# A hybrid attention, convolution and memory layer on eight cores: the first token blocks, the row sums' banks, the order of the key groups, and two seams

## The reference

```
z = x @ w_in                                  # q, k, v, f, g_fox, B, C, h, g_conv, mq, g_mem
logf = log_sigmoid(f + fox_bf)                # per head, 12 heads x 128
o_fox  = softmax(q.k/sqrt(128) + cum_t - cum_s, causal) @ v     # sample: 1024 cached keys before its own
o_conv = B * conv3(C * h)                     # causal, depthwise, 1536 channels, 2 steps of state
o_mem  = softmax(mq.mk/16) @ mv               # 4 heads x 256, 256 memory tokens
y_i = (o_i * silu(g_i)) @ w_i_out             # three branches
m = sum_i sigmoid(x @ w_merge_i + b_i) * y_i
y = LayerNorm(2**0.25 * x + m @ w_o)
```

## Time and profile before

| | us |
|---|---|
| median of 3 runs | 3396.12 (3395.94 to 3399.55) |
| profiled execution | 3396.83 |
| its span on the slowest core | 3395.1 |
| PE busy | 3283.1 (97%) |
| DVE, ACT, POOL busy | 1227.6, 906.3, 847.0 |
| mean granted PE clock, cores | 0.990 to 0.992 |

### The profile page before, as it was taken

The page is one execution under the profiler, slowest core; times in us unless marked ns, Lnnn a source line. Parts: engine busy times, 40 slices in busy tenths (PEclk is TensorE's granted clock), DMA queues, the critical chain, the costliest instruction groups (busy, mean ns, idle before and its releaser), DMA issues.

```text
span 3395.1 us, 54170 instructions; the slowest of 8 cores (3386.3 to 3395.1 us)
## 1 busy us (share of the span) xinstructions
PE 3283.1 (97%) x18645; PEld 1638.8 (48%) x18998; DVE 1227.6 (36%) x2041; ACT 906.3 (27%) x1572; POOL 847.0 (25%) x1046
## 2 busy tenths in 40 slices
PE   6999999999998999999999999999999999999998
PEld 3555555555544444444444444445544444444443
DVE  0477777777775222222211111111102331111465
ACT  0355555555553111111111111111113331111111
POOL 2233333333333222222200000222221113222233
PEclk8999999999999999999999999999999999999999
DMA  9554534343432121212134433866661115665543
GB/s 156 101 98 81 88 75 83 73 86 75 82 61 39 30 44 32 41 35 37 36 83 108 109 89 90 177 144 144 150 150 30 25 26 130 138 145 144 199 160 124
DMA packets 156405, 315.76 MB, mean 93 GB/s; under 512 B 32784, under 2 KB 60048, under 8 KB 151708
## 3 DMA queue, kind: packets, MB, share of 16 engines
q0 software_dynamic: 43840, 134.54, 24.1%
q1 hardware_dynamic: 112296, 177.73, 17.8%
HBM read 351.42 MB, written 95.32 MB: 132 GB/s over the span
## 4 chain that ended last, share of the span: by engine, by line
PE 92%; DMA 3%; issue 2%; DVE 1%; ACT 1%; POOL 0%; DVEq 0%; ACTq 0%; POOLq 0%; SPq 0%
PE bank L146 92%; DMA xT<-xTp 1%; DMA m_scr<-mt 1%; DVE st L181 0%; DMA fk_p<-k 0%; DVE acc L173 0%; ACT k L168 0%; DMA wcb<-wcM 0%; ACT rl L163 0%; DVE rr L181 0%; PE bank L149 0%; ACT sc L163 0%; ACT ge L163 0%; DVE pt L173 0%; POOL wv L155 0%
## 5 line engine op out<-in xcount | busy, mean ns | idle before, releaser
L146 PE MATMUL bank<-xT,wcb 128*128 128x512 bf16 (+1 forms) x3757 | 715.2, 342 | 9.8 <-DMA wcb<-wcM 4.7
L146 PE MATMUL bank<-xT,cwb 128*128 128x512 bf16 (+1 forms) x3766 | 693.9, 342 | 3.9 <-issue 0.2
L146 PE MATMUL bank<-xT,wkqg 128*128 128x512 bf16 (+1 forms) x2812 | 595.7, 344 | 18.3 <-DMA wkqg<-wkqg 5.9
L173 DVE TENSOR_TENSOR mt<-bank,gt 128x512 f32<-128x512 f32 (+1 forms) x240 | 143.6, 598 | 1033.8 <-PE bank L146 940.0
L146 PEld LDWEIGHTS bank<-xT,wcb 128*128 128x128 bf16 x3840 | 326.8, 98 | 366.9 <-issue 8.1
L146 PEld LDWEIGHTS bank<-xT,cwb 128*128 128x128 bf16 x3840 | 324.0, 98 | 362.4 <-issue 4.3
L163 ACT ACTIVATE pt<-st,ncc 128x512 bf16<-128x512 f32 (+4 forms) x492 | 318.7, 649 | 396.4 <-DVE st L181 306.6
L163 ACT ACTIVATE gt<-bank,bm 128x512 f32<-128x512 f32 (+1 forms) x240 | 147.1, 613 | 964.0 <-PE bank L146 959.8
L146 PEld LDWEIGHTS bank<-xT,wkqg 128*128 128x128 bf16 x2880 | 244.6, 98 | 270.7 <-issue 27.6
L181 DVE SCALAR_TENSOR_TENSOR st<-bank,cq 128x512 f32<-128x512 f32 x480 | 291.6, 608 | 172.0 <-PE bank L146 155.3
L173 DVE TENSOR_TENSOR acc<-acc,pt 128x512 f32<-128x512 f32 (+3 forms) x396 | 260.4, 658 | 0.4
(11 more groups left out here) (148 smaller groups left out, 2624.8 us busy)
## 6 DMA issues: line engine op xcount, KB each, us to landing
m_scr<-mt SPq DMA_DIRECT2D x128, 256.0 KB, 2.2
pv<-m_scr SPq DMA_DIRECT2D x128, 256.0 KB, 4.8
cwb<-wc POOLq DMA_DIRECT2D x10, 2048.0 KB, 15.1
mw<-wm POOLq DMA_DIRECT2D x16, 1024.0 KB, 12.2
x<-xp SPq DMA_DIRECT2D x16, 1024.0 KB, 7.0
y_p<-rr SPq DMA_DIRECT2D x16, 1024.0 KB, 4.8
wkqg<-wkqg POOLq DMA_DIRECT2D x40, 384.0 KB, 9.0
wcb<-wcC POOLq DMA_DIRECT2D x16, 896.0 KB, 9.0
```

The costliest lines, as they stand in the source:

```text
L146: return lambda e: e.matmul(out, lhsT=lhsT, rhs=rhs, start=start, stop=stop)
L173: return lambda e: e.tensor_tensor(out=out, in0=in0, in1=in1, op=op)
```

## The change

- Start: blocks 0 and 1 are both computed in seven banks side by side (four v groups, k, q, g), a quarter of the contraction at a time. The weights of head 0's k, q, g come in quarters, each behind the quarter of block 0; blocks 1 and 2 come in quarters. The constants go out from SP behind block 0, the later ones behind block 1; `identb` is dropped, `bfb` has a resource of its own.
- Row sums take their bank from `nextbank()`.
- The groups of the next head have a new order: one or no v group ahead of each, and key groups not next to each other.
- The copy of the sample's conv state goes from POOL to DVE.
- At the end of attention the low part of the last row sum and the first projection group of channel group 1 are put out before the row sum.
- In the last combine the order of the last two items' units is changed.

```diff
-    for t, n in ((identb, "identb"), (identf, "identf"), (onesb, "onesb")):
-        S.add(SP, DMA(t[:], I[n]), writes=[r_const], dmasem=dconst)
...
+    def load_const():
+        for t, n in ((identf, "identf"), (onesb, "onesb")):
+            S.add(SP, DMA(t[:], I[n]), writes=[r_const], dmasem=dconst)
+        S.add(SP, DMA(lcT[:, 0:PAST], I["clfT"]), writes=[r_lc], dmasem=d_clf)
+
+    def load_late():
+        for t, n in ((bm, "b_merge"), (cwT, "conv_w"), (cbT, "conv_b"), (sconvT, "sconv")):
+            S.add(SP, DMA(t[:], I[n]), writes=[r_late], dmasem=dlate)
...
         load_x(0, g, g + 1, S.dmasem(f"x0g{g}"))
-    for g in range(0, 4, 2):
-        load_kw(0, g, g + 2, S.dmasem(f"k0g{g}"))
-    for g in range(0, 4, 2):
-        load_x(1, g, g + 2, S.dmasem(f"x1g{g}"))
-    load_x(2, 0, 2, S.dmasem("x2a"))
-    load_x(2, 2, 4, S.dmasem("x2b"))
+        load_kw(0, g, g + 1, S.dmasem(f"k0g{g}"))
+    for tb in (1, 2):
+        for g in range(4):
+            load_x(tb, g, g + 1, S.dmasem(f"x{tb}g{g}"))
...
+    def stream_block(tb):
+        gs = [(2 + j, v_group(0, tb * 4 + j, True)) for j in range(4)]
+        gs += [(0, k_group(0, tb, True)), (1, q_group(0, tb, raw=True)), (7, g_group(0, tb, raw=True))]
+        for g in range(4):
+            for bk, (mm, ev) in gs:
+                for c in range(g * 4, g * 4 + 4):
+                    mm(bk, c, c == 0, c == 15)
+        for bk, (mm, ev) in gs:
+            ev(bk)
+    stream_block(0)
+    load_const()
+    stream_block(1)
+    load_late()
+    for tc in range(8, 12):
+        run_all(v_group(0, tc))
+    run_all(k_group(0, 2) + q_group(0, 2) + g_group(0, 2))
...
-                    lb = 2 + take("s", 2)
+                    lb = nextbank()
...
-                    S.add(POOL, COPY(conv["us"][:, 0:2], sconvT[:, :, c]), reads=[r_late], writes=[r_us])
+                    S.add(DVE, COPY(conv["us"][:, 0:2], sconvT[:, :, c]), reads=[r_late], writes=[r_us])
...
-            rest = []
-            for tb in (1, 2, 3, 4):
-                if h > 0 or tb > 2:
-                    rest.append(k_group(n, tb))
-                if tb == 1:
-                    rest += [g_group(n, 0, past_block[0]), q_group(n, 1, past_block[1]), g_group(n, 1, past_block[1])]
-            nv = (len(vs) // 4 + len(rest) - 1) // len(rest)
-            for grp in rest:
-                fill += vs[:4 * nv] + grp
-                vs = vs[4 * nv:]
-            assert not vs
-            fill += q_group(n, 4) + g_group(n, 4)
-            for tb in (2, 3):
-                fill += q_group(n, tb, past_block[tb]) + g_group(n, tb, past_block[tb])
+            rest = [k_group(n, 1)] if h > 0 else []
+            rest += [g_group(n, 0, past_block[0]), q_group(n, 1, past_block[1])]
+            rest += [k_group(n, 2)] if h > 0 else []
+            rest += [g_group(n, 1, past_block[1]), k_group(n, 3), q_group(n, 4), g_group(n, 4)]
+            nv, nr = len(vs) // 4, len(rest)
+            for k, grp in enumerate(rest):
+                fill += vs[4 * (nv * k // nr):4 * (nv * (k + 1) // nr)] + grp
+            fill += q_group(n, 2, past_block[2]) + k_group(n, 4) + g_group(n, 2, past_block[2])
+            fill += q_group(n, 3, past_block[3]) + g_group(n, 3, past_block[3])
...
-    for due, fn in later:
+    now[0] = None
+    ps = conv_pieces(1, True)
+    later[0][1]()
+    run_all(ps[:4])
+    for due, fn in later[1:]:
         fn()
...
+    units = [(k, tb) for k in range(len(ITEMS) - 2) for tb in range(5)]
+    ka, kb = len(ITEMS) - 2, len(ITEMS) - 1
+    units += [(ka, 0), (ka, 1), (kb, 0), (ka, 2), (kb, 1), (ka, 3), (kb, 2), (ka, 4), (kb, 3), (kb, 4)]
```

More of the change, by code:

```diff
@@ L217 @@
     ("wo", [4, 128, 16, 512], F32), ("ln_g", [1, D], F32), ("ln_b", [1, D], F32),
-    ("identb", [128, 128], BF16), ("identf", [128, 128], F32), ("onesb", [128, 128], BF16),
+    ("identf", [128, 128], F32), ("onesb", [128, 128], BF16),
 ]
@@ L309, in build @@
     r_const = Res("const")
-    identb = B("identb", [128, 128], BF16, [r_const])
     onesb = B("onesb", [128, 128], BF16, [r_const])
     identf = B("identf", [128, 128], F32, [r_const])
-    bfb = B("bfb", [128, H], F32, [r_const])
+    r_bfb = Res("bfb")
+    bfb = B("bfb", [128, H], F32, [r_bfb])
     r_one = Res("ones1")
@@ L342, in build @@
     S.add(DVE, lambda e: e.memset(ftm[:], 0.0), writes=[r_ftm])
-    for t, n in ((identb, "identb"), (identf, "identf"), (onesb, "onesb")):
-        S.add(SP, DMA(t[:], I[n]), writes=[r_const], dmasem=dconst)
-    S.add(SP, DMA(bfb[:], I["fox_bf"].partition_broadcast(128)), writes=[r_const], dmasem=dconst)
+    S.add(SP, DMA(bfb[:], I["fox_bf"].partition_broadcast(128)), writes=[r_bfb], dmasem=S.dmasem("bfb"))
     O_W0, O_CW0, O_CW1 = Z, Z + 14336, Z + 30720
@@ L420, in build @@
     d_clf = S.dmasem("clf")
-    S.add(SP, DMA(lcT[:, 0:PAST], I["clfT"]), writes=[r_lc], dmasem=d_clf)
-    for t, n in ((bm, "b_merge"), (cwT, "conv_w"), (cbT, "conv_b"), (sconvT, "sconv")):
-        S.add(SP, DMA(t[:], I[n]), writes=[r_late], dmasem=dlate)
+    def load_const():
[5 more added lines that the diff above has]
+            S.add(SP, DMA(t[:], I[n]), writes=[r_late], dmasem=dlate)
     CAP = 8192
@@ L461, in build @@
     pj = [0]
+    busy_banks = set()
     def nextbank():
@@ L465, in nextbank @@
         pj[0] += 1
+        assert b not in busy_banks
         return b
@@ L474, in fn @@
                     st["b"] = nextbank()
+                    busy_banks.add(st["b"])
                 for c in range(c0, c0 + step):
@@ L477, in fn @@
                 if c0 + step == n:
+                    busy_banks.discard(st["b"])
                     evict(st["b"])
@@ L502, in evict @@
                 S.add(DVE, TT(ftm[0:tn, tc, :], banks[bk][0:tn, 256:268], bfb[0:tn, :], ALU.add),
-                      reads=[bankr[bk], r_const], writes=[r_ftm])
+                      reads=[bankr[bk], r_bfb], writes=[r_ftm])
             if j == 1 or tc == 16:
@@ L522, in wmm, with k_group @@
         return mm
-    def k_group(h, tb):
+    def k_group(h, tb, raw=False):
         p = h % 2
@@ L534, in evict, with q_group @@
             S.add(SP, DMA(dst, k32[s][:, 0:tn]), reads=[r_k32[s]], dmasem=d_k32[s])
+        if raw:
+            return wmm(h, 0, tb), evict
         return group(wmm(h, 0, tb), tn, evict)
-    def q_group(h, tb, need=-1):
+    def q_group(h, tb, need=-1, raw=False):
         t0, tn = TBLK[tb]
@@ L546, in evict @@
                 S.add(ACT if h == 0 else DVE, COPY(qs[h % 2][:], banks[bk][:, 0:tn]), reads=[bankr[bk]], writes=[r_qs[h % 2]])
+        if raw:
+            return wmm(h, 1, tb), evict
         return group(wmm(h, 1, tb), tn, evict, need=need)
@@ L566, in silu_exp, with g_group @@
             later.append((now[0] + 2, gate))
-    def g_group(h, tb, need=-1):
+    def g_group(h, tb, need=-1, raw=False):
         t0, tn = TBLK[tb]
@@ L577, in evict @@
                 silu_exp(bk, tn, sgs[h % 2][:], r_sgs[h % 2])
+        if raw:
+            return wmm(h, 2, tb), evict
         return group(wmm(h, 2, tb), tn, evict, need=need)
@@ L1048, in build @@
     for c in range(1, 12):
-        ps = conv_pieces(c, True)
-        run_all(ps[:16])
+        if c > 1:
+            ps = conv_pieces(c, True)
+        run_all(ps[4 if c == 1 else 0:16])
         if c + 1 < 12:
@@ L1478, in make_in_maps @@
     f = lambda a: np.ascontiguousarray(np.asarray(a, dtype=np.float32))
-    identb = np.eye(128, dtype=np.float32).astype(ml_dtypes.bfloat16)
     identf = np.eye(128, dtype=np.float32)
@@ L1512, in make_in_maps @@
         "ln_g": f(inputs["ln_g"][0]).reshape(1, D), "ln_b": f(inputs["ln_b"][0]).reshape(1, D),
-        "identb": identb, "identf": identf, "onesb": onesb,
+        "identf": identf, "onesb": onesb,
     }
```

1 line of the change is left out of this document (removed).

## The result

The changed kernel took 3358.1 and 3359.9 us, against 3396.4 us (median of four); two more of its runs had a die at a lower clock and are left out, as such runs are below. That is a ratio of 0.9888 with a 95% interval of 0.9864 to 0.9912, some 37.5 us less. Forecast were 3354.0 us and a range of 3343 to 3371. The profiled execution took 3359.92 us, its slowest core 3358.4.

What follows compares the result with a forecast made beforehand. The prediction took TensorE (PE), 92% of the chain, as the bound, through its idle and half-clock time. Six gains, 6.1 + 13.0 + 6.3 + 5.0 + 5.3 + 6.4 = 42.1 us, gave a median of 3354.0 us, range 3343 to 3371.

Steps and rivals of the forecast that it cites:

- start: Blocks 0 and 1 streamed over seven banks as their chunks land: gain 6.1 us, ends 2 and 8.
- row sums: In attention, row sums in projection banks end most waits for `rl` and `st`: gain 13.0 us, ends 0 and 19.6.
- key groups: In the head without v groups, separating key groups removes a 3.43 us PE wait and slow clock: gain 6.3 us.
- conv state: In the last head, the copy on VectorE shortens PE's 4.17 us wait: gain 5.0 us, ends 3 and 5.9.
- the moved constants ... so nothing is late: Start: constants sent behind block 0's and 1's stores are first read 40 us and more later, so nothing is late.
- I take zero with 1 us as the other end: Start: cost of the eviction burst and of block 1's v32 slot held by its store, 0 to 1 us.
- the landing of block 3's input: Start: the last half lands at 88.9 us, set by the bytes on full DMA engines, unchanged ahead of each tile.
- rival one: Behind row sums, VectorE holds the burst back just as long, losing the 13.0 us: 3367.0 us; chance 0.18.
- The two seams: End of attention, gain 5.3 us, and last combine, gain 6.4 us: PE's waits and half clock there shrink.
- The signs: Expected afterwards: block 3's v groups end near 97 us, `rl` and `wcM` waits gone, clock at least 0.95 in attention.
- Transfer latency: Start: each of six more transfers adds its own latency, 10.2 us, block 3's input at 99.1: 3364.2 us; chance 0.08.
- The slower rival: Row sums take a bank from the projections, whose groups then wait: 81.6 us over 48 row sums, 3435.6 us; chance 0.05.

Runs made afterwards that it cites:

- undo_rows: The changed kernel with row sums back in the two score banks; ratio 0.9930 to the kernel before, attention 12.2 us longer than in the changed kernel.
- six_slots: The changed kernel with six v32 slots instead of two during the start; ratio 0.9883 to the kernel before, first score matmul at 125.9 us.
- two_banks: The changed kernel with two banks for all projection groups and bank 7 for row sums alone; ratio 1.0017 to the kernel before, attention 920.1 us.
- only_us: The kernel before with only the conv state copy moved from POOL to DVE; ratio 0.9993 to the kernel before, attention 933.9 us.

## Why the forecast was right in the whole, wrong in one term, and lucky in part

| term | forecast | measured alone |
|---|---|---|
| start | 6.1 | 1.5 (-1.9 by undo_rows) |
| row sums | 13.0 | 14.3 (12.2 undone) |
| key groups | 6.3 | 9.6 |
| conv state | 5.0 | 4.6 |
| end of attention | 5.3 | 4.9 |
| last combine | 6.4 | 6.2 |
| output projection | 0 | -0.7 |
| sum | 42.1 | 40.4 |

The whole gave 39.4 on the median core and about 37.5 in time. The key groups gave 3.3 us more than forecast and the row sums 1.3; that the total came so near in spite of the start is in part luck.

- **The start is the term that failed**, by 4.6 us or more; that is about the difference between 3354 and 3359. The step was "the moved constants ... so nothing is late". I asked when their readers come, and not what is queued behind them on SP's ring: constants with 1054 small packets under full DMA engines, then the stores that free the v32 slots (20.2 us to their landing, 9.5 with the constants in front).

  "I take zero with 1 us as the other end" for these slots was wrong with them: DVE waited 17 us, and PE 2.5 us for DVE on core 4 and 5.6 on the slowest. On core 4 block 3 began at 86.4, so its v groups could have ended at 95.8, sooner than the forecast's 97.4; they ended at 100.1, by 2.5 us of wait and 1.8 of matmuls below full clock behind it.

  The second step that failed is the landing of block 3's input. I held it fixed at 88.9 us of core 4. It is 78.1 on the median core with the stores held back, and between 86.1 and 90.4 in all other runs, old start or new: loads and stores share full engines, and I kept only the loads in the account. six_slots, where nobody waits for a store, still starts at 125.9.

  One more size was off without effect: block 1 was through at 58.8 us and not at 65 to 67, because block 0 ended at 41.0 and not at 45 to 47.3. Block 2 had to wait for its input all the same.
- **The row sums** went as forecast in their waits: between 200 and 940 us 19.6 us of waits for `rl` and `st` became 6.4 of `st`, where I had left 6.6. The forecast's reading that these waits "leave the clock at 1.00" was wrong: some cost 1.7 us of clock each, 2.4 us of the 14.3. VectorE as the bound (rival one) is what remains, not what takes the gain.
- **The key groups** were right in the place named and incomplete elsewhere: the first head and four with nine v chunks are at least 1.0 us shorter each, and the wait tables show a third of that. The waits for `ge`, which the forecast left out, went too.
- **The conv state** was right in size and wrong in what is left: 2.58 us for DVE where the forecast had 0.9 for POOL. That the size came out is luck as far as the runs show.
- **The two seams** were right within 0.4 us each, the half clock behind the waits included; that is closer than such marks repeat.
- **The signs.** `rl` is gone, `st` grew by 1.2 us between 200 and 940, and no wait over 3 us is left from 200 to 1070 us. Not so: the v groups of block 3 ended at 100.0 on the median core and not near 97; the clock is 0.83 over 10 us at 1000 on cores 4 and 5; and the wait for `wcM` is gone on four cores of eight.
- **The rivals.** Transfer latency: the six further transfers cost no time of their own that shows. The last quarter of block 3's input comes at 85.6 us in the changed kernel, sooner than 88.9 before, on core 4; the rival had it at 99.1. On the median core it is 86.1 against 87.6. The Trainium skill's "DMA: Bandwidth & Descriptors" (Anatomy of one DMA) gives about 2 us of fixed cost for each transfer, an estimated 12 us for six. No such delay shows in this case, where the engines are full (share 1.02 from 61 to 91 us on core 0). The slower rival: its mechanism is real, as two_banks shows, at 6.6 us of attention with every group at the short distance, not 82.

The single parts sum to 40.4 and the whole to 39.4. The row sums came out 2.1 us smaller with the new order of the groups, 12.2 for 14.3; that is little more than such marks differ by.

## What to carry to other kernels

When transfers are moved, list every queue they join and what stands behind them there: seven constants of 6 to 64 KB, put among the loads, held the store behind them for some 10 us longer once the engines were full. Where the engines are full, put loads and stores in one account, and hold back those that nobody waits for: the start became 10.0 us shorter than before that way, and 3.4 us by streaming and more slots alone (six_slots). A pool of banks shared by two kinds of work was cheap here, where evictions are done two groups later; look at the places with small groups. Short waits that come in pairs are worth a look at the clock behind them, too.

## What the runs showed of the hardware that I had not expected

- On core 0 a transfer of 12 KB in small pieces (the conv state) took 9.4 us to land when issued at 6.4 us and 30.5 us when issued at 61 us, with a DMA share of 1.0 in both; behind it a store of 256 KB took 20.5 us, and 10.0 with the constants out of the way.
- Shorter waits than I thought can cost clock, and not each time. Behind the 2.58 us wait in the last head the clock was 1.00 on the slowest core of the changed kernel, but 0.83 over 10 us on its cores 4 and 5 and on the slowest core of only_us. Behind the 2.15 us wait for `k` on core 2 before, four matmuls took 1.59 us instead of 1.03. And in the middle of attention one head of the kernel before is 1.7 us longer than its like (81.1 for 79.4 us on core 2), behind the row sum waits of 0.58 and 1.46 us shown above for core 4. What makes one such pair of waits cost clock and the next one not stays open.
- The output projection is 0.7 us longer with the streamed start (249.6 to 250.1 in seven profiles) than without it (248.9 to 249.0 in seven), though its own code is the same. That is open.
